# A decoder layer on one core: where the gate, projection and output weights are requested, what the router multiplies, and the order inside the expert loop

## The reference, cut to what matters

```python
def layer(x, ...):                       # 1024 prompt rows and 8 sample rows, D_MODEL = 1024, float32
    h = rmsnorm(x, norm_mix)
    ... = split_projection(h, w_in)      # q/k/v of both mixers; mg_a, mg_b are two gates of 1024 columns
    o_a = nsa(...)                       # sparse attention, 512 columns; prompt rows, then the 8 sample rows
    o_b = deltanet(...)                  # 512 columns
    mixed = sigmoid(mg_a) * (o_a @ w_proj_a) + sigmoid(mg_b) * (o_b @ w_proj_b)
    x = x + mixed @ w_out                # 1024 x 1024
    hf = rmsnorm(x, norm_ffn)            # x * rsqrt(mean(x*x) + eps) * norm_ffn
    group = argmax(hf @ w_router_g + b_g)             # 4 groups
    top2 of (hf @ w_router_e + b_e) inside the group  # 8 experts each, 32 in all
    return x + sum over the two experts of weight * ((silu(hf @ w_gate[e]) * (hf @ w_up[e])) @ w_down[e])
```

## Time and profile before

| | |
|---|---|
| median of 3 executions | 2845.91 us (2845.04 to 2850.43) |
| the profiled execution, its own time | 2846.74 us |
| its span in the profile | 2845.0 us |
| mean granted clock of PE, as a share of 2.4 GHz | 0.932 |
| busy: PE, DVE, ACT, POOL | 2515.7, 784.1, 493.2, 485.7 us |
| expert loop, `gate_and_up` (1024 records) | 450.6 us busy, 17.0 us idle before them |
| expert loop, `down` (512 records) | 225.0 us busy, 1.2 us idle before them |
| moved over DMA | 331.25 MB |

### The profile page before, as it was taken

The page is one execution under the profiler, slowest core; times in us unless marked ns, Lnnn a source line. Parts: engine busy times, 40 slices in busy tenths (PEclk is TensorE's granted clock), DMA queues, the critical chain, the costliest instruction groups (busy, mean ns, idle before and its releaser), DMA issues. The chain is left out here.

```text
span 2845.0 us, 32921 instructions
## 1 busy us (share of the span) xinstructions
PE 2515.7 (88%) x12051; PEld 1571.1 (55%) x12051; DVE 784.1 (28%) x1523; ACT 493.2 (17%) x1315; POOL 485.7 (17%) x574
## 2 busy tenths in 40 slices
PE   6999998999779999869816999979779999999996
PEld 4446655888566676647514666634334444444443
DVE  2016442555355655424420000001221111111110
ACT  1101111333024444423200000001100000000000
POOL 1035121343130000100030000011102112211221
PEclk8999999999569999979958999989879999999998
DMA  4010300000220000056255000032258888888894
GB/s 130 30 59 30 127 2 0 1 1 1 63 32 1 1 1 1 13 151 172 68 148 148 30 1 1 0 128 77 107 198 312 313 310 309 318 312 303 310 318 127
DMA packets 186148, 331.25 MB, mean 116 GB/s; under 512 B 32901, under 2 KB 82318, under 8 KB 185822
## 3 DMA queue, kind: packets, MB, share of 16 engines
q1 hardware_dynamic: 160118, 293.08, 30.4%
q0 software_dynamic: 15472, 28.89, 3.6%
q10 hardware_dynamic: 10432, 7.57, 0.9%
HBM read 307.48 MB, written 51.37 MB: 126 GB/s over the span
## 5 line engine op out<-in xcount | busy, mean ns | idle before, releaser
L2385 PE MATMUL psum<-f_W,f_xT 128*128 128x512 f32 x1024 | 450.6, 598 | 17.0 <-DVE f_xT L2431 16.0
L2385 PEld LDWEIGHTS psum<-f_W,f_xT 128*128 128x128 f32 x1024 | 193.0, 191 | 255.8 <-issue 254.6
L1918 PE MATMUL psum<-hT,x_wg 128*128 128x344 f32 x768 | 227.8, 455 | 20.7 <-DMA x_wg<-w_in 20.7
L419 PE MATMUL psum<-w,hT 128*128 128x512 f32 (+3 forms) x576 | 225.5, 552 | 7.1 <-DMA w<-w_in 7.1
L2395 PE MATMUL psum<-f_W,f_aT 128*128 128x512 f32 x512 | 225.0, 592 | 1.2 <-DVE f_aT L2446 1.2
L1918 PEld LDWEIGHTS psum<-hT,x_wg 128*128 128x128 f32 x768 | 146.8, 191 | 97.5 <-DMA x_wg<-w_in 20.8
L419 PEld LDWEIGHTS psum<-w,hT 128*128 128x128 f32 (+1 forms) x576 | 103.6, 182 | 122.7 <-issue 107.6
L419 PE MATMUL psum<-hT,w 128*128 128x344 f32 x576 | 168.9, 454 | 0.0
L2395 PEld LDWEIGHTS psum<-f_W,f_aT 128*128 128x128 f32 x512 | 97.2, 190 | 123.4 <-issue 123.4
L1491 ACT ACTIVATE a_P<-psum,a_nmax 128x512 f32<-128x512 f32 (+4 forms) x256 | 123.0, 494 | 168.5 <-DVE a_nmax L1420 109.2
L2435 DVE TENSOR_TENSOR f_a<-f_sg,psum 128x512 f32<-128x512 f32 x32 | 22.0, 689 | 460.7 <-ACT f_sg L2416 460.7
(11 more groups left out here) (481 smaller groups left out, 3429.6 us busy)
## 6 DMA issues: line engine op xcount, KB each, us to landing
f_W<-w_gate SPq DMA_DIRECT2D x32, 2048.0 KB, 14.2
f_W<-w_up SPq DMA_DIRECT2D x32, 2048.0 KB, 20.3
f_W<-w_down SPq DMA_DIRECT2D x32, 2048.0 KB, 9.5
k_stage<-cache_nsa SPq DMA_DIRECT2D x128, 192.0 KB, 2.6
w<-w_in SPq DMA_DIRECT2D x6, 2048.0 KB, 7.9
x_wg<-w_in SPq DMA_DIRECT2D x8, 1024.0 KB, 13.7
x<-x_prompt SPq DMA_DIRECT2D x8, 512.0 KB, 4.4
o_x<-x_prompt SPq DMA_DIRECT2D x8, 512.0 KB, 4.3
```

The source lines that it names most:

```text
L419: ins = nc.tensor.matmul(PS[i % 4][0:m_rows, 0:n], lhsT, rhs, start=(k == 0), stop=(k == KD - 1))
L1918: ins = nc.tensor.matmul(PS[b + i][:, 0:n], wg[q % 3][:, k, i, c:c + P], hT[:, k, t0:t0 + n], start=(k == 0), stop=(k == KD - 1))
L2385: ins = nc.tensor.matmul(PS[bank][:, :], xT[par][:, k, :], w[par][:, k, :], start=(k == 0), stop=(k == KD - 1))
```

## The change

1. In sample attention, SP waits for the first half (`o_done`) and then asks for the first quarter of the gate weights and for `x_wa`; both lie where `b_vlo` was. `x_wb` moves to `A_DN`. PE waits for `x_wa` and `x_wb` apart.
2. In the merge, SP asks for `w_out` in two halves after units 12 and 18, into the buffers of gate quarters 1 and 2. The output stage no longer asks for it.
3. In the output stage, PE transposes `x1` and not `h2`, as soon as `x1` is there. The router weights are multiplied once by `norm_ffn` (a table `gk`, on DVE), and `r` is applied when the products leave PSUM. `h2` is still made and stored for the experts. `x1` has three buffers and not nine, so DVE waits for the buffer of three tiles ago.
4. In the experts, the first 32 blocks run without tests; the loop with tests for blocks 32 to 47 stands behind one test of the count. The row transposes of block b + 1 move from `rest` to the end of `first`, so on PE they come before `down` of block b - 1 and not behind it; their copies on ACT and DVE move in the same way. POOL's functions are as before.

```diff
@@ sample attention, SP
+            sp.wait_ge(o_done, 1)
+            load_gate_weights(sp, w_in, 0, wg, g_loaded)
+            for g in range(2):
+                sp.dma_start(wa[64 * g:64 * g + 64, :, :], w_a[256 * g:256 * g + 256].rearrange("(j d) n -> d j n", d=HD)).then_inc(wa_loaded, 16)
@@ merge, SP
-            for g in range(2):
-                sp.dma_start(wa[64 * g:64 * g + 64, :, :], w_a[256 * g:256 * g + 256].rearrange("(j d) n -> d j n", d=HD)).then_inc(wab_loaded, 16)
-            for q in range(4):
-                if q == 1:
-                    sp.dma_start(wb[:, :, :], w_b.rearrange("(j p) n -> p j n", p=P)).then_inc(wab_loaded, 16)
+            sp.dma_start(wb[:, :, :], w_b.rearrange("(j p) n -> p j n", p=P)).then_inc(wb_loaded, 16)
+            for q in range(1, 4):
                 if q >= 3:
                     sp.wait_ge(mm_done, 6 * (q - 2))
...
+                load_gate_weights(sp, w_in, q, wg, g_loaded)
+            for i in range(2):
+                sp.wait_ge(mm_done, 6 * (i + 2))
+                sp.dma_start(wo[i][:, :, :], w_out[512 * i:512 * i + 512].rearrange("(k p) n -> p k n", p=P)).then_inc(wo_loaded, 16)
@@ output stage, SP and PE
-                    sp.dma_start(wo[:, :, :], w_out.rearrange("(k p) n -> p k n", p=P)).then_inc(w_loaded, 16)
...
+                    sp.dma_start(gk[:, :], norm_ffn.rearrange("(k p) -> p k", p=P), allow_slow_non_contiguous=True).then_inc(small_loaded, 16)
...
-                pe.wait_ge(h2_done, t + 1)
+                pe.wait_ge(x1_done, t + 1)
                 if t >= 1:
-                    pe.wait_ge(h2T_done, t)
+                    pe.wait_ge(x1T_done, t)
@@ output stage, DVE
-                nc.vector.tensor_tensor(logits[0:n, t, :], PS[6 + t % 2][0:n, 0:NG + NE], bias[0:n, :], ALU.add).then_inc(lg_copied, 1)
+                nc.vector.scalar_tensor_tensor(logits[0:n, t, :], PS[6 + t % 2][0:n, 0:NG + NE], r[0:n, t:t + 1], bias[0:n, :], ALU.mult, ALU.add).then_inc(lg_copied, 1)
...
+            nc.vector.tensor_tensor(wr[:, :, :], wr[:, :, :], gk[:, :].unsqueeze(2).to_broadcast([P, KD, NG + NE]), ALU.mult).then_inc(scaled, 1)
...
+                if t >= 3:
+                    dve.wait_ge(sq_done, t - 2)
+                    dve.wait_ge(tp_done, t - 2)
+                    dve.wait_ge(x1_stored[t % 3], 16 * (t // 3))
@@ experts, every engine
-            with engine.Fori(0, MAXBLK // 2) as i:
-                for par, b, number in ((1, 2 * i + 1, i + 1), (0, 2 * i + 2, i + 2)):
-                    with engine.If(b < n):
-                        first(par, number, i + 2, b)
...
+            def step(b, par, i):
+                first(par, i + 1 if par else i + 2, i + 2, b)
+                tail(1 - par, i + 1)
+                rest(par, i + 1 if par else i + 2, i + 2)
+
+            with engine.Fori(0, NE // 2 - 1) as i:
+                step(2 * i + 1, 1, i)
+                step(2 * i + 2, 0, i)
+            step(NE - 1, 1, NE // 2 - 1)
+            with engine.If(n < NE + 1):
+                tail(1, NE // 2)
+            with engine.If(n > NE):
+                with engine.Fori(NE // 2, MAXBLK // 2) as i:
...
@@ experts, PE
                     for k in range(KD):
                         ins = nc.tensor.matmul(PS[bank][:, :], xT[par][:, k, :], w[par][:, k, :], start=(k == 0), stop=(k == KD - 1))
                 ins.then_inc(gu_done[par], 1)
+                transpose_rows(1 - par, u_next)
...
             def transposes(par, u, u_next):
-                transpose_rows(1 - par, u_next)
                 pe.wait_ge(a_done[par], u)
@@ experts, ACT (DVE alike)
                 nc.scalar.activation(sg[:, :], PS[2][:, :], ACT.Silu).then_inc(silu_done[par], 1)
+                copy_rows(1 - par, u_next)
```

More of the change, by code:

```diff
@@ L1883, in block_merge @@
         sem = L.signals.named("x_")
[L1884 to L1887, removed]
+        wb_loaded, mm_done, sig_done, t_done, m_done = map(sem, ("wb_loaded", "mm", "sig", "t", "m"))
+        wb = L.at("x_wb", A_DN, [P, 4, D])
         T = Region(L, A_R + 32768, A_R + 41856)
         sg = [T(f"x_sig{i}", [P, 2, 512]) for i in range(2)]
-        wg = [L.at(f"x_wg{i}", A_DN + 16384 * i, [P, KD, 2, 256]) for i in range(3)]
-        wv = w_in.rearrange("(k p) n -> p k n", p=P)
         units = [(m, t0, n) for m in range(KD) for t0, n in THIRDS]
@@ L1918, in _ @@
                         ins = nc.tensor.matmul(PS[b + i][:, 0:n], wg[q % 3][:, k, i, c:c + P], hT[:, k, t0:t0 + n], start=(k == 0), stop=(k == KD - 1))
-                if u == 0:
-                    pe.wait_ge(wab_loaded, 48)
-                for i, (w, o) in enumerate(((wa, oaT), (wb, obT))):
+                for i, (w, o, loaded, count) in enumerate(((wa, oaT, wa_loaded, 32), (wb, obT, wb_loaded, 16))):
+                    if u == 0:
+                        pe.wait_ge(loaded, count)
                     for k in range(4):
@@ L2070, in _ @@
                 for half in range(2):
-                    ins = nc.scalar.copy(h2T[:, t % 2, 4 * half:4 * half + 4, 0:n], PS[4 + half][:, :].rearrange("p (k n) -> p k n", k=4)[:, :, 0:n])
-                ins.then_inc(h2T_done, 1)
-            act.wait_ge(x1_stored, 16 * (NT + 1))
+                    ins = nc.scalar.copy(x1T[:, t % 2, 4 * half:4 * half + 4, 0:n], PS[4 + half][:, :].rearrange("p (k n) -> p k n", k=4)[:, :, 0:n])
+                ins.then_inc(x1T_done, 1)
+            for s in x1_stored:
+                act.wait_ge(s, 16 * 3)
         @block.gpsimd
         def _(pool):
-            pool.wait_ge(small_loaded, 80)
+            pool.wait_ge(small_loaded, 96)
             for t, n in tiles:
@@ L2294, in each_block @@
             first, tail, rest = first or nothing, tail or nothing, rest or nothing
-            n = engine.value_load(blocks[0:1, MAXBLK:MAXBLK + 1], min_val=MINBLK, max_val=MAXBLK)
+            n = engine.value_load(blocks[0:1, MAXBLK:MAXBLK + 1], min_val=NE, max_val=MAXBLK)
             first(0, 1, 1, 0)
             rest(0, 1, 1)
-            with engine.Fori(0, MAXBLK // 2) as i:
-                for par, b, number in ((1, 2 * i + 1, i + 1), (0, 2 * i + 2, i + 2)):
-                    with engine.If(b < n):
-                        first(par, number, i + 2, b)
[L2302 to L2305, removed]
-                        with engine.If(b < n):
-                            rest(par, number, i + 2)
+            def step(b, par, i):
[10 more added lines that the diff above has]
+                with engine.Fori(NE // 2, MAXBLK // 2) as i:
+                    for par, b, number in ((0, 2 * i, i + 1), (1, 2 * i + 1, i + 1)):
+                        with engine.If(b < n):
+                            first(par, number, i + 1 + par, b)
+                        if tail is not nothing:
+                            with engine.If(b < n + 1):
+                                tail(1 - par, i + par)
+                        if rest is not nothing:
+                            with engine.If(b < n):
+                                rest(par, number, i + 1 + par)
+                if tail is not nothing:
+                    with engine.If(n > MAXBLK - 1):
+                        tail(1, MAXBLK // 2)
             return n
@@ L2319, in load @@
             def load(par, u, u_next, b):
-                if isinstance(b, int):
+                if isinstance(b, int) and b == 0:
                     return
@@ L2424, in _ @@
             copy_rows(0, 1)
-            each_block(act, silu, copy_out, lambda par, u, u_next: copy_rows(1 - par, u_next))
+            each_block(act, silu, copy_out)
         @block.vector
@@ L2500, in build @@
     sw = L.at("sw", A_OA - 2080, [64, WIN + 1])
+    wg = [L.at(f"x_wg{i}", at, [P, KD, 2, 256]) for i, at in enumerate((A_R, A_DN + 16384, A_DN + 32768))]
+    wa = L.at("x_wa", A_R + 16384, [P, 4, D])
+    wo = [L.at(f"o_w{i}", at, [P, 4, D]) for i, at in enumerate((A_DN + 16384, A_DN + 32768))]
+    g_loaded = [nc.alloc_semaphore(f"g_loaded{i}") for i in range(3)]
+    wa_loaded, wo_loaded = nc.alloc_semaphore("wa_loaded"), nc.alloc_semaphore("wo_loaded")
     block_window_keys(nc, L, PS, C, rows(I["state_win"][0]), I["page_table"], qT, kT, gates_s, qbd, snew, g64, pages, sw)
```

69 lines of the change are left out of this document (35 added, 34 removed).

## The result

The changed kernel takes 3040.7 us (median of 4 runs, 3039.15 to 3044.14) against 2847.8 us for the kernel before beside it (4 runs, 2845.04 to 2850.43): a ratio of 1.068, with a 95% interval of 1.066 to 1.070. It is 193 us slower. The profiled execution has a span of 3038.4 us against 2845.0, with a mean granted clock of 0.909 against 0.932.

What follows compares the result with a forecast made beforehand. PE's work and stands were taken to bound the kernel. Gather stalls 177, clock 60, earlier merge requests -16.0, `w_out` -14.2, loop end -8.4 and -0.9 sum to +197.5 us: 3043 us, range 2975 to 3097.

Steps and rivals of the forecast that it cites:

- T: In the expert loop, the moment when `down` of a block ends and the next piece of PE's list begins.
- Which scatter the gather waits for: Expert loop: gather of block b + 1 is behind the scatter of block b - 2; PE stands 6.6 us.
- The string: POOL's list per expert step: second add, wait for its landing, index copy, gather; rows land at T + 20.9 us.
- The step's length: Expert loop: a step at full clock grows from 22.70 to 28.6 us, 5.9 us more.
- The clock: Expert loop: granted clock falls in every stand, costing 2.0 us a step, 60 us in all (ends 0 and 110).
- Rival 1: Expert loop: the clock stays up despite PE's stands; 2983 us, chance 0.08.
- Rival 2: Expert loop: clock comes back late, 2.5 to 3.66 us lost per step; 3073 us, at most 3093, chance 0.12.
- Thirty steps: Expert loop: rows 3 to 32 are fetched behind a scatter, so 30 steps lose 5.9 us each, 177 us.
- The requests: Seams: merge weights asked for earlier, PE starts at 1510, net -16.0 us; `w_out` fetched within the merge, -14.2 us.
- Rival 4: Stage seams: requests gain nothing, since what is fetched early delays what is fetched next; 3073 us, chance 0.05.
- Router and loop end: Output stage: router from `x1` gains 0; expert loop's end: empty rounds go, -8.4 us, last `down` waits less, -0.9.
- Rival 3: Expert loop: no stall, the gather is there when PE wants it; 2787 or 2797 us, chance 0.07.

## Why the prediction was right

The forecast of 3043 us met 3040.7, and its steps held one by one, with the exceptions named below. The two traces give a ledger of +193.4 us of span (predicted: +197.5):

| stretch | predicted | measured |
|---|---|---|
| merge starts earlier, net of what is given back | -16.0 | -14.3 |
| `w_out` | -14.2 | -14.2 |
| rest up to T of block 0: output stage, routing, first block | 0 | -0.8 |
| 30 steps of the loop | +237 | +231.8 |
| from the last T to the end | -9.3 | -9.0 |

**Which scatter the gather waits for.** Right, and it is the step on which all hangs. The landing was forecast at T + 20.9 and came at T + 20.86 in the step shown, and between T + 19.6 and T + 21.7 in all 29; the stand was forecast at 6.6, and it was 6.55 on average. The string's parts kept their lengths within 0.3 us although the DMA share of the loop fell from 0.88 to 0.66. The other half, that it is POOL's order and not the transfer that is late, was implied by the string and is now shown: with the wait moved, the rows are there at T + 14.5.

**The step's length.** 28.6 at full clock was forecast; with the stand filled by transposes the 29 steps ahead of the last average 28.66 (858.21 us from the first T to the last, less 27.16 for the last step).

**The clock.** 2.0 a step was taken, between 0 and 3.66. The changed kernel's 29 steps average 30.64 us (912.93 less 24.26), so the clock cost 30.64 - 28.66 = 1.98. That a fall would come was reasoned; that its price came out within 0.02 was luck, since the row it leaned on had 1.56 and the other 3.66. Rival 1 (the clock stays up) fell with the windows. Rival 2 (it comes back late, 2.5 to 3.66) fell with the price, and with the twin filled by transposes. The rule behind it is in the Trainium skill ("TensorE: Matmul & The Clock Gate", Part 4: PE-mode transpose), by which transposes don't count as busy as products do. By that rule the twin would have taken 3040 us or more; the measured 2994.68 speaks against it for these float32 transposes, as the rows of the first stage did. The empty stand alone tells the two apart less well: the lower clock went on for some 4.1 us behind it, over the 8 transposes and 2.3 us of `down`, where the prediction's reading of the rule had some 3.

**Thirty steps.** This was the term that was off by most. The last of the 30 is only 24.26 us, 1.6 above a step of before: of the weights only `w_down` is still fetched beside it (issued at 2990.84), its adds and its gather land sooner (the gather in 4.1 us, 3003.03 to 3007.10, and not in 7.0), and PE stands 2.1 us. By steps: 29 x 7.94 + 1.6 = 231.8, where 30 x 7.9 = 237 had been put.

**The requests.** The first product was forecast at 1510 and came at 1510.96. Of the 16.2 us gained the first unit's gate products gave back 1.3 (12.53 us against 11.23), since they ran at the lower clock for the first 6.1 us and not 3.5, and the late `x_wb` gave back 0.6, of which PE stood 0.30; 1.1 had been put for `x_wb` and nothing for the clock. Rival 4 (fetched early delays what comes next) shows in that 0.6 and is no more than that. `w_out` gave its 14.2.

**Router and loop end.** The router edit at 0 is confirmed by the trace of a kernel that has `h2` again. One reading under it was off: `h2` was ready at 1952.9 in a middle tile and PE took it at 1965.1, some 12 us later and not 6, which leaves the 0 as it was. Routing itself was 1.5 us shorter (38.34 against 39.88, from PE's first product in it to its first row transpose); 1.1 of it is in its 36 products, which took 6.61 us against 7.73. They took 7.64 in the kernel with requests and router edit alone, and 6.61 in the one with `h2` again, so it goes with neither edit. The granted clock accounts for it: after some 10 us in which PE stood, it was 0.50 for the first 4.6 us of these products where they took 6.61, and for the first 7 where they took 7.6 or 7.7. Why it came back sooner in two of the four stays open. The end came out at -9.0 against -9.3.

**Rival 3.** No stall was wrong for this kernel, but its price was right for one that lacks the stall: 2787 to 2797, and the kernel with the earlier gather takes 2794.5.

**The signs.** Those that the prediction named came: 28 of the 30 steps take 30 to 31.1 us, the loop's DMA share is 0.66 (about 0.65 forecast), and the merge's first product starts 2.9 us behind SP's first request of that stage (1508.08; 2 to 3 forecast).

## What to carry to other kernels

An instruction moved ahead of other work asks for its data earlier by the whole length of that work. Before moving it, work out from the timeline when the data land, counted from the event that releases their fetch, and compare that with the new time of asking: a landing with 1.8 us to spare became 6.6 us late, and moving the fetch ahead as well (one block further ahead in POOL's list) turned a loss of 193 us into a gain of 52, of which 38 belong to the other parts of the change and 14 to the loop. Look through the list of the engine that issues the fetch for waits that the fetch itself does not need.

Price a stand of TensorE at more than its length: in 29 steps, 6.6 us of standing took 2.0 us more on average in the work behind it.

## What the runs showed of the hardware

Transposes alone, 5.4 us of them in each stand, kept the granted clock at 1.00 over the whole loop; with six products of 128x512 (5.3 us) in the same place it fell in three steps, those with the longest stands left (2.03 to 2.38 us).

The two adds and the gather, all on POOL's software queue, overlap: issued with both adds in flight the rows took 8.1 us instead of 7.0 (median of 33 in either kernel), and the adds landed 8.8 us after the second one's start (2393.39 to 2402.20) instead of 9.0 (2410.66 to 2419.65). The Trainium skill ("DMA: Bandwidth & Descriptors", Anatomy of one DMA — SWDGE (gpsimd) path) has a fit of 2.0 us and the bytes at 436 GB/s. As an estimate from it, 512 KB, the size of such a gather, would take 3.2 us; beside the expert weights, and as 128 rows by index, they took 7.0 here, so the measurement is the one to plan with. In the last of the 30 steps, with a DMA share of 0.35 beside it and not 0.94, the gather took 4.1 us; that gather is for block 32, which this data leaves empty, so how much of the distance is traffic is not shown.

A stand's length and its cost in clock can be told apart by filling it with work whose results nobody uses.
